# An mLSTM tile with its denominators in a matmul group of their own and its normaliser steps batched over heads

## The reference, cut to what matters

```python
s = jnp.einsum('bhntd,bhnsd->bhnts', q, k) * dec
num = jnp.einsum('bhnts,bhnse->bhnte', s, v) + inter[..., None] * jnp.einsum('bhntd,bhnde->bhnte', q, c0)
den = jnp.sum(s, axis=-1) + inter * jnp.einsum('bhntd,bhnd->bhnt', q, n0)
hid = num / jnp.maximum(jnp.abs(den), jnp.exp(-m_t))[..., None]
...
hid = h_f + flip(h_b) if return_h else None
...
hn = h * lax.rsqrt(jnp.mean(h * h, axis=-1, keepdims=True) + EPS)
hn = hn.transpose(0, 2, 1, 3).reshape(b, l, MLSTM_W) * gain.astype(jnp.float32)
return (hn * jax.nn.sigmoid(o.astype(jnp.float32))).astype(o.dtype)
```

## Time and profile before

| what | us |
|---|---|
| median of 9 runs (lowest to highest) | 1351.05 (1345.43 to 1421.69) |
| the profiled execution, its own time | 1349.3 |
| its span, on the slowest core | 1347.6 |
| busy: PE, DVE, ACT, POOL, in the whole span | 938.5, 724.8, 570.9, 290.3 |

### The profile page before, as it was taken

How to read it: one execution, slowest core, us unless ns; L and a number is a source line. 1 busy time by engine, 2 the same in 40 slices (tenths; PEclk the granted TensorE clock), 3 DMA queues, 4 the chain that set the end, 5 groups by cost and what they waited for, 6 DMA issues and landing times.

```text
span 1347.6 us, 19147 instructions; the slowest of 8 cores (1331.7 to 1347.6 us)
## 1 busy us (share of the span) xinstructions
PE 938.5 (70%) x5284; PEld 465.4 (35%) x5352; DVE 724.8 (54%) x1520; ACT 570.9 (42%) x1190; POOL 290.3 (22%) x283
## 2 busy tenths in 40 slices
PE   0235936776685666656554757979998998989984
PEld 0222414332233333333322323434443443434431
DVE  0581674024565555555521575666567468466668
ACT  2472781255515555555420443440441340441456
POOL 1000003000044434433230542330220130230200
PEclk9999979878885655555586987989999998999998
DMA  9544100420000000800096334440451250440405
GB/s 191 144 126 63 18 1 4 60 32 1 0 1 1 2 1 1 126 1 2 1 210 118 110 69 46 51 47 1 48 55 16 32 60 4 47 47 1 48 32 219
DMA packets 73412, 68.62 MB, mean 51 GB/s; under 512 B 48096, under 2 KB 58336, under 8 KB 73056
## 3 DMA queue, kind: packets, MB, share of 16 engines
q0 software_dynamic: 64528, 37.79, 21.6%
q1 hardware_dynamic: 8784, 29.61, 6.6%
HBM read 96.78 MB, written 8.39 MB: 78 GB/s over the span
## 4 chain that ended last, share of the span: by engine, by line
PE 35%; DVE 23%; ACT 18%; issue 13%; DMA 9%; DVEq 1%; POOL 1%; ACTq 0%; SPq 0%; POOLq 0%
PE ps L1244 8%; PE ps L1205 6%; PE ps L641 6%; DVE facc L1228 4%; PE ps L1221 4%; DVE facc L1226 3%; DMA wabg<-w_ada 3%; ACT pTb L898 3%; PE ps L1134 3%; DMA wab<-w_ada 2%; ACT fth L1230 2%; DVE gT L1231 2%; ACT asb L1208 2%; DMA wib<-w_in 2%; PE ps L895 2%
## 5 line engine op out<-in xcount | busy, mean ns | idle before, releaser
L1244 PE MATMUL ps<-wdb,gT 128*128 128x512 bf16 x689 | 165.8, 399 | 33.4 <-DVE gT L1231 23.7
L1221 PE MATMUL ps<-actT,wub 128*128 128x512 bf16 x691 | 155.8, 379 | 6.3 <-DVE gT L1231 5.6
L1205 PE MATMUL ps<-actT,wub 128*128 128x512 bf16 x689 | 156.6, 383 | 1.0 <-issue 0.2
L1230 ACT ACTIVATE fth<-facc 128x512 f32<-128x512 f32 x88 | 55.4, 629 | 176.7 <-DVE facc L1228 176.7
L641 PE MATMUL ps<-wib,actT 128*128 128x512 bf16 (+1 forms) x502 | 120.5, 396 | 3.0 <-DVE rt L667 0.5
L1249 DVE TENSOR_TENSOR x<-ps,x 128x512 f32<-128x512 f32 x160 | 104.8, 687 | 21.7 <-PE ps L1244 21.4
L1244 PEld LDWEIGHTS ps<-wdb,gT 128*128 128x128 bf16 x704 | 70.0, 102 | 129.3 <-issue 58.3
L1226 DVE SCALAR_TENSOR_TENSOR facc<-asb,ffcw,facc 128x512 f32<-128x512 f32 x88 | 68.9, 783 | 74.8 <-ACT facc L1224 74.2
L1231 DVE TENSOR_TENSOR gT<-fth,ps 128x512 bf16<-128x512 f32 x88 | 60.6, 688 | 80.8 <-ACT fth L1230 68.8
L1208 ACT COPY asb<-ps 128x512 f32<-128x512 f32 x88 | 46.3, 592 | 133.2 <-PE ps L1205 130.6
L898 ACT ACTIVATE pTb<-ps 128x512 bf16<-128x512 f32 x156 | 84.8, 639 | 38.0 <-PE ps L895 38.0
(11 more groups left out here) (184 smaller groups left out, 1396.7 us busy)
## 6 DMA issues: line engine op xcount, KB each, us to landing
wub<-w_up POOLq DMA_DIRECT2D x44, 256.0 KB, 4.7
xbuf<-x SPq DMA_DIRECT2D x16, 512.0 KB, 3.8
xb<-x SPq DMA_DIRECT2D x16, 512.0 KB, 3.5
out<-x SPq DMA_DIRECT2D x16, 512.0 KB, 2.7
wabg<-w_ada POOLq DMA_DIRECT2D x3, 2048.0 KB, 23.7
wdb<-w_down POOLq DMA_DIRECT2D x22, 256.0 KB, 5.0
wib<-w_in POOLq DMA_DIRECT2D x5, 1024.0 KB, 13.1
wab<-w_ada POOLq DMA_DIRECT2D x2, 2048.0 KB, 27.3
```

Source lines behind the costliest of these rows:

```text
L1205: ins = e.matmul(ps[b][:, :], wub[i2][:, k, 0:128], actT[:, k, tg * 512:(tg + 1) * 512], start=(k == 0), stop=(k == KC - 1))
L1221: ins = e.matmul(ps[bv][:, :], wub[i2][:, k, 128:256], actT[:, k, p0:p0 + 512], start=(k == 0), stop=(k == KC - 1))
L1230: kb.op("act", lambda e: e.activation(ft[:], fa[:], AF.Gelu_apprx_tanh), reads=[("facc", j2)], writes=[("fth", j2)])
L1244: ins = e.matmul(ps[b][:, :], gT[:, cgi - c0, T * 128:(T + 1) * 128], wdb[:, cgi % NRING, half * 512:(half + 1) * 512], start=(cgi == c0), ...
```

## The change

Three edits in `mlstm_tile`, and one wait list in `finish_tile`:

- The 129th column leaves the numerators. A new step (turn 3) computes the denominators of both directions and all four heads as 16 matmuls with one moving column into one PSUM bank, and the normaliser for all eight (head, direction) pairs with three DVE instructions on 8 columns in place of twelve on 2.
- The numerators of one direction go to one bank (8 matmuls of 128 columns). The backward ones (turn 4) are scaled by one DVE instruction of 512 columns into `hsum`, in place of four on ACT; the backward state update, which had a turn of its own, follows in the same turn, ahead of that turn's attention pair. The forward ones (turn 5) are scaled by one DVE instruction into `hsq`, and POOL adds `hsq` to `hsum`, in place of four DVE instructions.
- The norm over heads comes in turn 6, ahead of that turn's attention pair and of the next tile's first turn; its two products of 512 columns become four fused DVE instructions of 128 columns, one for each head.

The attention steps keep their turns, and a tile still starts every five turns.

```diff
--- before.py
+++ after.py
@@ -957,46 +957,58 @@
         hs = hsum[i2]
         while T < NT - 1 and not su_done.get(T + 1, False):
             yield
+        bd = kb.bank()
+
+        def mmd(e):
+            ins = None
+            for d_ in range(2):
+                iv = ivf if d_ == 0 else ivb
+                for h in range(4):
+                    o = ps[bd][:, d_ * 4 + h:d_ * 4 + h + 1]
+                    e.matmul(o, sTm[d_][i2][:, h, :], vwb[d_][iv][:, h, 128:129], start=True, stop=False)
+                    c0 = C0(T)[:, h, 128:129] if d_ == 0 else Cbf[:, 1, h, 128:129]
+                    ins = e.matmul(o, qT[:, h, T * 128:(T + 1) * 128], c0, start=False, stop=True)
+            return ins
+        ckeys = [C0K(T, 0), C0K(T, 1), ("Cbf", 1, 0), ("Cbf", 1, 1)]
+        vkeys = [("vwb", 0, ivf, h) for h in range(4)] + [("vwb", 1, ivb, h) for h in range(4)]
+        kb.op("pe", mmd, reads=[("sTm", 0, i2), ("sTm", 1, i2)] + ckeys + vkeys + qk_keys, writes=[PS(bd)])
+        fa = fsm[:, i2, 0, 0:8]
+        fb = fsm[:, i2, 1, 0:8]
+        kb.op("dve", lambda e: e.tensor_tensor(fa, ps[bd][:, 0:8], gd[:, 0, ti, :, :].rearrange("p d h -> p (d h)"), ALU.max),
+              reads=[PS(bd), ("gd", 0, 0), ("gd", 0, 1)], writes=[("fsm", i2, 0)])
+        kb.op("dve", lambda e: e.scalar_tensor_tensor(fb, ps[bd][:, 0:8], -1.0, fa, ALU.mult, ALU.max),
+              reads=[PS(bd), ("fsm", i2, 0)], writes=[("fsm", i2, 1)])
+        kb.op("dve", lambda e: e.reciprocal(fb, fb), reads=[("fsm", i2, 1)], writes=[("fsm", i2, 1)])
+        yield
         for idx_, d_ in enumerate((1, 0)):
             iv = ivf if d_ == 0 else ivb
-            for p_ in range(2):
-                b = kb.bank()
-
-                def mmp(e, b=b, d_=d_, p_=p_, iv=iv):
-                    ins = None
-                    for hh in range(2):
-                        h = 2 * p_ + hh
-                        o = ps[b][:, hh * 129:(hh + 1) * 129]
-                        e.matmul(o, sTm[d_][i2][:, h, :], vwb[d_][iv][:, h, :], start=True, stop=False)
-                        c0 = C0(T)[:, h, :] if d_ == 0 else Cbf[:, 1, h, :]
-                        ins = e.matmul(o, qT[:, h, T * 128:(T + 1) * 128], c0, start=False, stop=True)
-                    return ins
-                ckey = C0K(T, p_) if d_ == 0 else ("Cbf", 1, p_)
-                kb.op("pe", mmp, reads=[("sTm", d_, i2), ckey] + [("vwb", d_, iv, h) for h in range(4)] + qk_keys, writes=[PS(b)])
-                p3 = ps[b][:, 0:258].rearrange("p (h e) -> p h e", e=129)
-                fa = fsm[:, i2, d_ * 2 + p_, 0:2]
-                fb = fsm[:, i2, 4 + d_ * 2 + p_, 0:2]
-                fkey = ("fsm", i2, d_ * 2 + p_)
-                kb.op("dve", lambda e, p3=p3, fa=fa, d_=d_, p_=p_: e.tensor_tensor(fa, p3[:, :, 128], gd[:, 0, ti, d_, 2 * p_:2 * p_ + 2], ALU.max),
-                      reads=[PS(b), ("gd", 0, d_)], writes=[fkey])
-                kb.op("dve", lambda e, p3=p3, fa=fa, fb=fb: e.scalar_tensor_tensor(fb, p3[:, :, 128], -1.0, fa, ALU.mult, ALU.max),
-                      reads=[PS(b), fkey], writes=[("fsm", i2, 4 + d_ * 2 + p_)])
-                kb.op("dve", lambda e, fb=fb: e.reciprocal(fb, fb), reads=[("fsm", i2, 4 + d_ * 2 + p_)], writes=[("fsm", i2, 4 + d_ * 2 + p_)])
-                for hh in range(2):
-                    h = 2 * p_ + hh
-                    if idx_ == 0:
-                        kb.op("act", lambda e, p3=p3, fb=fb, hh=hh, h=h: e.activation(hs[:, h, :], p3[:, hh, 0:128], AF.Copy, scale=fb[:, hh:hh + 1]),
-                              reads=[PS(b), ("fsm", i2, 4 + d_ * 2 + p_)], writes=[("hsum", i2, h)])
-                    else:
-                        kb.op("dve", lambda e, p3=p3, fb=fb, hh=hh, h=h: e.scalar_tensor_tensor(hs[:, h, :], p3[:, hh, 0:128], fb[:, hh:hh + 1], hs[:, h, :],
-                                                                                             ALU.mult, ALU.add),
-                              reads=[PS(b), ("fsm", i2, 4 + d_ * 2 + p_), ("hsum", i2, h)], writes=[("hsum", i2, h)])
-                yield
-            if d_ == 1:
+            b = kb.bank()
+
+            def mmp(e, b=b, d_=d_, iv=iv):
+                ins = None
+                for h in range(4):
+                    o = ps[b][:, h * 128:(h + 1) * 128]
+                    e.matmul(o, sTm[d_][i2][:, h, :], vwb[d_][iv][:, h, 0:128], start=True, stop=False)
+                    c0 = C0(T)[:, h, 0:128] if d_ == 0 else Cbf[:, 1, h, 0:128]
+                    ins = e.matmul(o, qT[:, h, T * 128:(T + 1) * 128], c0, start=False, stop=True)
+                return ins
+            ck = [C0K(T, 0), C0K(T, 1)] if d_ == 0 else [("Cbf", 1, 0), ("Cbf", 1, 1)]
+            kb.op("pe", mmp, reads=[("sTm", d_, i2)] + ck + [("vwb", d_, iv, h) for h in range(4)] + qk_keys, writes=[PS(b)])
+            p3 = ps[b][:, :].rearrange("p (h e) -> p h e", e=128)
+            fbc = fb[:, 4 * d_:4 * d_ + 4].unsqueeze(2).to_broadcast([128, 4, 128])
+            if idx_ == 0:
+                kb.op("dve", lambda e, p3=p3, fbc=fbc: e.tensor_tensor(hs[:], p3, fbc, ALU.mult),
+                      reads=[PS(b), ("fsm", i2, 1)], writes=[("hsum", i2, h) for h in range(4)])
                 if T > 0:
                     state_update(ti, 1, ik, ivb, cp="act")
                 su_done[T] = True
-                yield
+            else:
+                hq = hsqs[i2]
+                kb.op("dve", lambda e, p3=p3, fbc=fbc, hq=hq: e.tensor_tensor(hq[:], p3, fbc, ALU.mult),
+                      reads=[PS(b), ("fsm", i2, 1)], writes=[("hsq", i2)])
+                kb.op("pool", lambda e, hq=hq: e.tensor_tensor(hs[:], hs[:], hq[:], ALU.add),
+                      reads=[("hsq", i2)] + [("hsum", i2, h) for h in range(4)], writes=[("hsum", i2, h) for h in range(4)])
+            yield
         HK = [("hsum", i2, h) for h in range(4)]
         hsq = hsqs[i2]
         kb.op("act", lambda e: e.activation(hsq[:], hs[:], AF.Square), reads=HK, writes=[("hsq", i2)])
@@ -1004,10 +1016,10 @@
         kb.op("dve", lambda e: e.tensor_reduce(ssq, hsq[:], AX.X, ALU.add), reads=[("hsq", i2)], writes=[("fsm", i2, 10)])
         kb.op("act", lambda e: e.activation(ssq, ssq, AF.Ln, scale=1.0 / 128, bias=epsb[:, 0:1]), reads=[("fsm", i2, 10), "epsb"], writes=[("fsm", i2, 10)])
         kb.op("act", lambda e: e.activation(ssq, ssq, AF.Exp, scale=-0.5), reads=[("fsm", i2, 10)], writes=[("fsm", i2, 10)])
-        kb.op("dve", lambda e: e.tensor_tensor(hsq[:], hs[:], ssq.unsqueeze(2).to_broadcast([128, 4, 128]), ALU.mult),
-              reads=HK + [("fsm", i2, 10)], writes=[("hsq", i2)])
-        kb.op("dve", lambda e: e.tensor_tensor(yt[:, 0:512], hsq[:].rearrange("p h d -> p (h d)"), OG(T), ALU.mult),
-              reads=[("hsq", i2), OGK(T)], writes=[ykey + ("m",)])
+        for h in range(4):
+            kb.op("dve", lambda e, h=h: e.scalar_tensor_tensor(yt[:, h * 128:(h + 1) * 128], hs[:, h, :], ssq[:, h:h + 1],
+                                                               OG(T)[:, h * 128:(h + 1) * 128], ALU.mult, ALU.mult),
+                  reads=HK + [("fsm", i2, 10), OGK(T)], writes=[ykey + ("m", h)])
         yield
 
     su_done = {}
@@ -1022,7 +1034,7 @@
             for c in range(KC):
                 ins = e.transpose(psb[b][:, c * 128:(c + 1) * 128], yt[:, c * 128:(c + 1) * 128], identb[:])
             return ins
-        kb.op("pe", try_, reads=[ykey + ("m",), ykey + ("a", 0), ykey + ("a", 1), "identb"], writes=[PS(b)])
+        kb.op("pe", try_, reads=[ykey + ("m", h_) for h_ in range(4)] + [ykey + ("a", 0), ykey + ("a", 1), "identb"], writes=[PS(b)])
         kb.op("act", lambda e: e.copy(actT[:, :, T * 128:(T + 1) * 128], psb[b][:, :].rearrange("p (c t) -> p c t", c=KC)),
               reads=[PS(b)], writes=AT(T))
 
```

## The result

The changed kernel takes 1367.86 us (median of 10 runs, 1365.08 to 1402.99) beside 1350.58 for the kernel before (32 runs): a ratio of 1.0122, 95% interval 1.0098 to 1.0146. It is slower, by about half of the forecast of 32 us. The profiled execution took 1365.76 us.

The account below looks back on a forecast made before the run. The bound was the longest round trip through the engines' program-order queues, 16.50 us per tile. The new one summed to 18.85: +30.6 over 13 tiles, +1.7 at the tail, +32.3 on 1349.3, so 1381.6; range 1368 to 1403.

Parts of the forecast that it names:

- Step 1: From the start of the older tile's square to the end of the norm's exponential on ACT: 2.11 us.
- step 2: Block 4's first exponential to the start of attention output 0, mask included: 2.33 us, reaching 4.48 with 0.04 of start.
- steps 3 to 6: Attention output 0 through DVE's copies, denominators, score pair and transposes to the backward numerators' reader: from 4.48 to 11.49 us.
- steps 7 and 8: DVE's backward scaling 0.69, four state steps 1.83, hand-over 0.13, second cast 0.30: block 2's exponentials start at 14.44.
- step 9: Block 2's exponentials to its masks 0.79, both masks on POOL 2.26: reaching 17.49, with the forward scaling hidden.
- step 10: POOL's add 1.26 behind the masks, hand-over to ACT 0.10: next square at 18.85, ACT stalling 2.5 us before it.
- steps 4 to 6: On PE: denominators 0.6, score pair 0.54, eight transposes 0.80, eight backward numerators 0.75 plus 0.43 us.
- the tail: From the square of tile 1 to the last transposes, 19.02 us before: transposes start near 20.7, +1.7.
- Removed work pays: ACT's reciprocal wait and scalings: 1.9 us leave the round trip, 14 tiles give -27, so 1322; chance 0.09.
- POOL's tail is hidden: Block 2's masks and the add end by 16.36, when ACT arrives: beat 16.4, time 1350; chance 0.09.
- heavier than the sum: One-column matmuls cost 1.0, add 1.64, hand-overs high: 1.0 to 1.2 more per tile, up to 1403; chance 0.16.
- The rule on contention: DVE's fused products overlap block 4's first mask on POOL: possibly 0.5 us more per tile, near 1389; not in the sum.

Follow-up runs that it names:

- the third kernel of the clock's group: Kernel before plus seven unread 512-column matmuls per tile on PE ahead of its transposes: 1349.1 us, ratio 0.9997.
- the masks-first kernel: Changed kernel with the attention's masked key blocks taken first, nothing left out: 1317.14 us, ratio 0.9758.
- three of the kernels above: Changed kernel with the state update one turn later (1348.9); that plus the add on DVE (1349.14); masked key blocks first plus the add on DVE (1327.5).
- the kernel with both edits: Changed kernel with the add on DVE and the backward state update one turn later: 1349.14 us, ratio 1.0004.

## Why the prediction was right in kind and wrong in size

**The mechanism held.** The square waits for POOL's add in all 13 tiles, 2.3 us each in the rows shown (forecast 2.5). The add follows the masks at once, the casts stand ahead of block 2's exponentials, PE's wait before the transposes is gone. Taking the add off POOL (1332.56), or the masks from in front of it (1330.68, 1317.14), turns the loss into a gain each time.

**Step by step, in the slow beat from 490.21.** Step 1 took 2.02 to the exponentials (2.15 with its 0.04 of start), step 2 2.22 (2.33), steps 3 to 6 from 494.45 to 501.49 7.04 (7.01), steps 7 and 8 from there to the exponentials 2.83 (2.95), step 9 to the add 2.95 (3.05), step 10 1.41 (1.36). The sum is 18.47 against 18.85. The unknown prices were met: the 16 denominators 0.50 with hand-over, 25 to 29 ns apart (0.6 taken), the add 1.26 (1.26 taken).

**What failed is the clock in steps 4 to 6.** I priced PE's work at its lower level of 1.2 GHz in all tiles, because the kernel before ran so the earlier trace rows. In five of the 13 beats of core 5 TensorE had its higher level of 2.4 GHz from the denominators to the backward scaling. The windows of that stretch in the two beats shown, the fast one first:

```profile
480.98:483.02 2.04, 2.04 (x40) 1.69 (x40) 0.96 (x5) 1.09 (x3) 0.00 (x0) 1.00 0.00 0
498.39:501.49 3.10, 3.10 (x38) 2.63 (x38) 1.02 (x5) 1.90 (x3) 0.00 (x0) 0.50 0.02 5
```

The transposes in it took 0.62 and not 1.04. Ahead of it, step 3 took 3.90 (477.08 to 480.98) and 3.94 (494.45 to 498.39); behind it, from the scaling to the square, both beats took 7.19. So the 1.1 us between 5.94 and 7.04 lie in steps 4 to 6 and nowhere else. It is so on all eight cores: 37 of their 104 beats have this stretch at a granted clock of 1.00 and take 17.4 to 17.7 us, 67 have it at 0.50 and take 18.4 to 18.9. On core 5, five times 1.07 (7.01 - 5.94) is 5.4 us; small differences, some 0.3 in each tile, about 0.1 each in step 1, step 2, steps 7 and 8, and step 9, are the other 3.8. Together 9.2, which is 13 x 18.85 less the 235.89 of core 5. The error in the reasoning is one of order: before, this stretch held a wait of 3.5 us on DVE, and the clock didn't matter (the third kernel of the clock's group). The change took that wait out, and by that put PE's own work on the path, where its clock counts. My low bound of 18.45 per tile had only hand-overs in it.

**Head and tail.** The head was taken as unmoved within -1.5 to +2.4 and came at -1.3. At the tail the clock decides again. On cores 4 and 5 the transposes came 20.6 after the square of tile 1, near the forecast of 20.7; on the other six they came after 19.0, as before (19.02). The windows of cores 5 and 6 from that square to the transposes, 0.58 and 0.68 in the clock:

```profile
672.67:693.25 20.58, 10.16 (x124) 7.70 (x125) 11.49 (x29) 9.46 (x19) 7.86 (x7) 0.58 0.00 1
672.62:691.60 18.98, 8.53 (x124) 6.61 (x125) 11.45 (x29) 9.25 (x19) 7.85 (x7) 0.68 0.01 1
```

In the mean the tail gave +0.4 and not +1.7. From the transposes to the end the cores took 1.3 us less in the mean (670.6 against 671.9). I didn't locate this; it is small beside the spread of the cores, 667.4 to 674.0. The start of the stage, which I didn't forecast, gave -0.8.

**The total.** In the means over the cores the beat came 8.9 under the forecast (30.6 to 21.7), the tail 1.3, what follows it 1.3, the head 1.3 and the start 0.8: 13.6 in all, which leads from +32.3 to +18.7. The clock is the largest term of it: 4.8 in the beats (37 fast ones on eight cores, each with 1.03 less than the 7.01 of steps 3 to 6) and 1.2 in the tail. The median lies just under the range's low end of 1368; without the clock's 6 us it would have been near 1374, inside the range. That end allowed half a us of overlap in each tile, a guess; a clock term of up to 1.1 us in each of 13 tiles, worked out from TensorE at its higher level, would have put it near 1361 (1375 - 14).

**The rivals.** "Removed work pays" named the right condition: if the add is done when ACT arrives, the removed work pays. In the changed kernel it isn't. Where the runs made it so, the removed work paid 18 to 21 us (1350.58 to 1332.56; 1338.17 to 1317.14), less than its 27. "POOL's tail is hidden" is refuted by the wait of 2.3 us, "heavier than the sum" by the two prices above. The 1399 and 1403 of that rival are also more than its own terms give: 1381.6 + 13 x 1.2 is 1397, and 1400 with the head.

**The rule on contention.** In the slow beat the four fused products took 2.98 us while POOL ran block 4's masks, and 1.14 in the masks-first kernel, where POOL was idle meanwhile. POOL's masks took 2.31 for two against 2.26 elsewhere. The Trainium skill, GPSIMD Engine Reference, Key points, names this contention; the trace agrees that it exists, and shows that here DVE pays most of it. By the rule I had put an estimated 0.5 us per tile on POOL; the measured price in the changed kernel is nothing, since the fused products end long before the transposes, and the kernel with two products (1370.63) shows that this spot isn't on the path. Where the held instruction is on the path, as L802 in three of the kernels above (1348.9, 1349.14, 1327.5), it costs time. For the second of these a run shows it (1323.36 without the masks); for the other two it is read from their rows.

## What to carry to other kernels

Price an instruction that moves to another engine by what stands ahead of it in that engine's queue, not by its own duration: here 1.26 us on POOL cost 35 us behind two masks and almost nothing once the masks stood earlier (1.2 us of waits in 13 tiles). When a change takes a wait out of a round trip, ask which engine's work comes onto the path in its place, and price that at each clock level that the trace shows. Before moving a DVE instruction with two SBUF operands, look at what POOL runs beside it in the new place: it waits for the end of that.

## What the runs showed of the hardware

A DVE instruction with both operands in SBUF that begins while POOL runs a mask or a v product waits for the end of it: L802 takes 427 to 430 ns alone, and beside POOL it ends 0.28 to 0.29 us after POOL's instruction, which makes 926 to 1106 ns in the mean and up to 1.36 us. The fused products took 2.98 us for four in place of 1.14. POOL pays less: a mask that begins while the held L802 still runs takes 1.33 us in place of 1.15, a v product 1.23 in place of 1.05. L799, with one operand in PSUM, stayed at 0.41 to 0.43, beside a mask too (497.03 in the kernel with both edits). Matmuls of one column follow each other in 25 to 30 ns at both levels of TensorE's clock, so a group of 16 is cheap at either. And the granted clock from the denominators to the scaling was 1.00 in some tiles and 0.50 in others with the same instructions. More work on PE ahead of it made the first kind more frequent (84 of 104 beats in place of 37); which of them a tile gets, these runs don't say.
